# Down product of both feed-forward layers as seven block products instead of eight, with operand sums made on GpSimd

## What is computed

```python
D_MODEL, SEQ = 1024, 1024
FFN_HIDDEN = -(-8 * D_MODEL // (3 * 256)) * 256      # 2816

def swiglu(u, w_gate, w_up, w_down):
    return (jax.nn.silu(u @ w_gate) * (u @ w_up)) @ w_down
...
x = x + mixer(rmsnorm(x, g0));  x = x + swiglu(rmsnorm(x, g1), w_gate, w_up, w_down)
```

## Time and profile before

| what | value |
|---|---|
| median of 3 runs | 2556.0 us (2555.74 to 2561.59) |
| the profiled execution: its time | 2557.84 us |
| the profiled execution: its span | 2556.1 us |
| granted TensorE clock, mean over the span | 0.984 |
| TensorE busy | 2486.2 us (97%) |
| VectorE busy | 1537.7 us (60%) |
| ScalarE busy | 1011.0 us (40%) |
| GpSimd busy | 216.8 us (8%) |
| down phase of layer 0 | from 1288.9 to 1533.4 us |
| down phase of layer 1 | from 2288.3 to 2534.1 us |
| gate and up phases | up to 1288.9 and up to 2288.3 us, 20 rounds each |

### The profile page before, as it was taken

One profiled execution on the slowest core, in us unless ns is written; L12 is line 12 of the kernel. 1 busy time (PEld: TensorE's weight loads), 2 busy tenths in 40 slices (PEclk: granted clock), 3 DMA queues, 4 the chain that ended last, 5 costly groups with the idle time before them and its releaser, 6 DMA issues.

```text
span 2556.1 us, 34009 instructions
## 1 busy us (share of the span) xinstructions
PE 2486.2 (97%) x13110; PEld 1960.9 (77%) x13110; DVE 1537.7 (60%) x2635; ACT 1011.0 (40%) x1818; POOL 216.8 (8%) x243
## 2 busy tenths in 40 slices
PE   9999999999999999999999999989999999999998
PEld 6587778865658788888888787776878888888787
DVE  5489967846635775666543637637676665653454
ACT  5423234545434433333332434537443333332333
POOL 4025524310000000000100000000000000000000
PEclk9999979999999999999999999999999999999999
DMA  6121100010004322232364341110332222236342
GB/s 191 41 75 42 50 9 11 2 34 1 1 26 146 125 80 78 83 94 72 103 224 147 133 130 34 41 50 26 91 123 83 83 83 83 83 126 220 116 161 103
DMA packets 207184, 217.54 MB, mean 85 GB/s; under 512 B 12496, under 2 KB 174304, under 8 KB 203568
## 3 DMA queue, kind: packets, MB, share of 16 engines
q1 hardware_dynamic: 204080, 196.13, 24.6%
q0 software_dynamic: 2944, 19.24, 2.1%
HBM read 172.35 MB, written 42.47 MB: 84 GB/s over the span
## 4 chain that ended last, share of the span: by engine, by line
PE 90%; DVE 5%; ACT 3%; issue 2%; POOL 0%; DVEq 0%; ACTq 0%; POOLq 0%
PE ps L335 25%; PE ps L337 24%; PE ps L336 24%; PE ps L2956 3%; PE ps L2933 2%; PE ps L2944 1%; DVE met L2081 1%; PE ps L2320 1%; ACT d_p L1591 1%; PE ps L2334 1%; PE ps L2329 1%; PE ps L1863 1%; PE ps L2373 1%; PE ps L2297 1%; PE ps L2382 1%
## 5 line engine op out<-in xcount | busy, mean ns | idle before, releaser
L324 DVE TENSOR_TENSOR wlo<-wraw,whi 128x1024 fp32r<-128x1024 f32 x152 | 186.3, 1228 | 370.5 <-ACT whi L318 370.1
L318 ACT ACTIVATE whi<-wraw 128x1024 fp32r<-128x1024 f32 x166 | 175.0, 1055 | 356.7 <-PE ps L337 339.2
L335 PE MATMUL ps<-ahi,whi 128*128 128x512 f32 x704 | 276.2, 392 | 6.4 <-DVE hT L962 4.1
L337 PE MATMUL ps<-ahi,wlo 128*128 128x512 f32 x704 | 274.9, 390 | 0.0
L336 PE MATMUL ps<-alo,whi 128*128 128x512 f32 x704 | 274.7, 390 | 0.0
L335 PE MATMUL ps<-uhi,whi 128*128 128x512 f32 x608 | 245.0, 403 | 6.5 <-DVE ulo L494 3.4
L335 PE MATMUL ps<-q_T,whi 128*128 128x512 f32 x640 | 249.4, 390 | 1.6 <-ACT upr L763 1.6
L337 PE MATMUL ps<-q_T,wlo 128*128 128x512 f32 x640 | 249.3, 389 | 0.0
L336 PE MATMUL ps<-q_T,whi 128*128 128x512 f32 x640 | 249.3, 389 | 0.0
L335 PE MATMUL ps<-q_B,whi 128*128 128x512 f32 x608 | 239.1, 393 | 2.4 <-DVE q_B L494 2.4
L336 PE MATMUL ps<-ulo,whi 128*128 128x512 f32 x608 | 237.3, 390 | 0.0
(11 more groups left out here) (465 smaller groups left out, 4517.5 us busy)
## 6 DMA issues: line engine op xcount, KB each, us to landing
wraw<-in_ffn_w_down_dram SPq DMA_DIRECT2D x88, 512.0 KB, 3.7
wraw<-in_ffn_w_gate_dram SPq DMA_DIRECT2D x44, 512.0 KB, 5.5
araw<-acts SPq DMA_DIRECT2D x88, 256.0 KB, 3.8
wraw<-in_ab_w_in_dram SPq DMA_DIRECT2D x24, 512.0 KB, 3.8
park<-hT POOLq DMA_DIRECT2D x3, 4096.0 KB, 12.3
wraw<-in_ffn_w_up_dram SPq DMA_DIRECT2D x24, 512.0 KB, 5.2
acts<-sgA SPq DMA_DIRECT2D x12, 1024.0 KB, 4.6
raw<-in_ffn_w_up_dram SPq DMA_DIRECT2D x20, 512.0 KB, 4.0
```

What stands on the lines that cost most here:

```text
L318: nc.scalar.activation(as_raw(whi[:, t.slot, :]), raw, ACT.Copy).then_inc(S("w_high"), 1)
L324: eng.tensor_tensor(as_raw(wlo[:, t.slot, :]), raw, as_raw(whi[:, t.slot, :]).bitcast(F32), ALU.subtract).then_inc(S("w_split"), 1)
L335: nc.tensor.matmul(dst, wh, xh, start=start, stop=False, **kw)
L337: return nc.tensor.matmul(dst, wl, xh, start=False, stop=stop, **kw)
```

## The change

The down product is cut in blocks: the hidden tiles into even and odd ones of each pair (`a`), the output features into a low and a high half, the tokens into two halves. Eight block products (2 x 2 x 2) become seven, listed in `DOWN`: which weight block or sum of blocks, which activation block or sum, which of two sets of four banks, whether the banks start from zero, and which quarter of `hT` the banks are added to. A step now holds two hidden tiles of one block product: 512 output features of each, so the weight tile is 128 x (2 x 512) and the activation tile grows from 512 to 2 x 512. There are 7 x 6 = 42 steps (`DT`) in each layer; every sixth has only one hidden tile and half the work. The activations' ring is three slots like the weights'.

The four sums of a pair's weights and the four of its activations are made by GpSimd (`ffn_sums`), 11 pairs in each layer, during the gate and up phase: the weights of the pair are loaded from DRAM once more, summed in place and stored to `w_sums`; the activations are summed in place in `sg[p % 2]` after their store to `acts`, and stored to `act_sums`. ScalarE's `sum_copy` into that buffer then waits for this second store (`sums_stored`). Block products 0 and 1 use plain operands, 2 to 4 sums on both sides, 5 and 6 a sum on one side. `park` is loaded back behind steps 3 to 10.

VectorE now adds banks to `hT` seven times four in each layer, each after the second step of the following block product; the one exception is the sixth and seventh block product, which use the same set of banks.

```diff
-    return order + [("down", layer, h, k) for h in range(2) for k in range(HT)]
+    return order + [("down", layer, i, c) for i in range(len(DOWN)) for c in range(DC)]
+DOWN = (
+    ((0, 1, 0), (0, 1, 1), 0, True, (0, 1)),
+    ((0, 0, 0), (0, 0, 1), 1, True, (0, 1)),
+    ((1, 1, 1), (1, 0, 1), 0, True, (1, 0)),
+    ((1, 0, 0), (1, 1, 0), 1, False, (0, 0)),
+    ((1, 1, 0), (0, 1, 0), 0, False, (0, 0)),
+    ((1, 0, 1), (1, 0, 0), 1, False, (1, 0)),
+    ((0, 1, 1), (1, 1, 1), 1, False, (1, 1)),
+)
...
+DC = (PAIRS + 1) // 2
+DT = len(DOWN) * DC
+DOWN_BANKS = ((6, 7, 0, 1), (2, 3, 4, 5))
+SAME_PIECE = {1: 0, 4: 3, 5: 2}
...
-        araw = at("araw", [P, 4, HALF], 32 * KB)
-        ahi = at("ahi", [P, 4, HALF], 40 * KB, F32R)
-        alo = at("alo", [P, 4, HALF], 48 * KB, F32R)
+        araw = at("araw", [P, RING, D], 32 * KB)
+        ahi = at("ahi", [P, RING, D], 44 * KB, F32R)
+        alo = at("alo", [P, RING, D], 188 * KB, F32R)
+        wd = at("wd", [P, 2, D], 176 * KB)
...
+            lo, hi = slice(0, HALF), slice(HALF, D)
+            pool.wait_ge(*after("t_lo", 16 * layer + 16))
+            for p in range(PAIRS):
+                if p:
+                    pool.wait_ge(*weights_summed(layer, p - 1))
+                pool.dma_start(wd[:, :, :], down_v[layer][:, p, :, :]).then_inc(S("wd_landed"), 16)
+                pool.wait_ge(*after("wd_landed", 16 * (PAIRS * layer + p + 1)))
+                add(wd[:, 1, hi], wd[:, 0, hi], wd[:, 1, hi], ALU.add)
+                add(wd[:, 0, hi], wd[:, 0, lo], wd[:, 0, hi], ALU.subtract)
+                add(wd[:, 0, lo], wd[:, 1, hi], wd[:, 0, lo], ALU.subtract, 2)
+                add(wd[:, 1, lo], wd[:, 1, lo], wd[:, 0, lo], ALU.subtract, 1)
+                pool.wait_ge(*after("p_sum", n[0]))
+                pool.dma_start(w_sums[:, p, :, :], wd[:, :, :]).then_inc(S("w_summed"), 16)
+                v = sg[p % 2]
+                pool.wait_ge(*act_stored(layer, p))
+                add(v[:, 0, hi], v[:, 0, lo], v[:, 0, hi], ALU.subtract)
+                add(v[:, 0, lo], v[:, 1, lo], v[:, 0, lo], ALU.subtract)
+                add(v[:, 1, lo], v[:, 1, lo], v[:, 0, hi], ALU.subtract, 2)
+                add(v[:, 1, hi], v[:, 1, hi], v[:, 1, lo], ALU.subtract, 1)
+                pool.wait_ge(*after("p_sum", n[0]))
+                pool.dma_start(act_sums[:, p, :, :], v[:, :, :]).then_inc(S(f"act_sums{p % 2}"), 16)
...
+                if w_sum:
+                    sp_.wait_ge(*weights_summed(layer, pairs[-1]))
+                sp_.wait_ge(S("w_split"), tile.n + 1)
+                src = w_sums if w_sum else down_v[layer]
+                sp_.dma_start(as_pairs(wraw[:, tile.slot, 0:width]),
+                              src[:, pairs[0]:pairs[-1] + 1, w_odd, w_half * HALF:(w_half + 1) * HALF]
+                              ).then_inc(S(f"w_landed{tile.slot}"), 16)
+                if n < RING:
                     sp_.wait_ge(*after("s_prod", NC * layer + AT[("A11", NJ - 1)] + 1))
                 else:
-                    sp_.wait_ge(*after("a_lo", 2 * HT * layer + n - 3))
-                p = k // 2
-                sp_.wait_ge(*act_stored(layer, p))
-                sp_.dma_start(araw[:, n % 4, :], acts[:, k, h * HALF:(h + 1) * HALF]).then_inc(S(f"a_landed{n % 4}"), 16)
+                    sp_.wait_ge(*after("a_lo", DT * layer + n - RING + 1))
+                for p in pairs:
+                    if a_sum:
+                        sp_.wait_ge(*sums_stored(layer, p))
+                    else:
+                        sp_.wait_ge(*act_stored(layer, p))
+                src = act_sums if a_sum else acts_v
+                sp_.dma_start(as_pairs(araw[:, n % RING, 0:width]),
+                              src[:, pairs[0]:pairs[-1] + 1, a_odd, a_half * HALF:(a_half + 1) * HALF]
+                              ).then_inc(S(f"a_landed{n % RING}"), 16)
                 if n == 2:
                     store(PAIRS - 1)
-                if 4 <= n < 4 + KT:
-                    if n == 4:
+                if 3 <= n < 3 + KT:
+                    if n == 3:
                         sp_.wait_ge(*after("s_prod", NC * layer + AT[("S3", NJ - 1)] + 1))
-                    sp_.dma_start(hT[:, n - 4, :], park[:, n - 4, :]).then_inc(S("h_again"), 16)
+                    sp_.dma_start(hT[:, n - 3, :], park[:, n - 3, :]).then_inc(S("h_again"), 16)
...
+                pe.wait_ge(*after("a_lo", DT * layer + n + 1))
+                for q in range(len(pairs)):
+                    if i == len(DOWN) - 1 and c == 1 and q == 1:
+                        norm_whole(pe, 2 * norm + 2, DOWN_BANKS[0][0])
+                    cols = slice(q * HALF, (q + 1) * HALF)
+                    for m in range(4):
+                        if c == 0 and q == 0 and earlier:
+                            pe.wait_ge(*after("d_added", 4 * len(DOWN) * layer + 4 * earlier[-1] + m + 1))
+                        elif c == 0 and q == 0 and (i, m) == (0, 2):
+                            pe.wait_ge(*out_count(layer, "C12", NJ - 2))
+                        elif c == 0 and q == 0 and (i, m) == (1, 0):
+                            pe.wait_ge(*out_count(layer, "C12", NJ - 1))
+                        w = slice(q * HALF + m * P, q * HALF + (m + 1) * P)
+                        last = three_pass(bank(banks[m]), whi[:, tile.slot, w], wlo[:, tile.slot, w],
+                                          ahi[:, n % RING, cols], alo[:, n % RING, cols],
+                                          start and c == 0 and q == 0, c == DC - 1 and q == len(pairs) - 1,
+                                          skip_group_check=True)
+                        if c == DC - 1 and m < 3:
+                            last.then_inc(S("d_part"), 1)
+                last.then_inc(S("w_used"), 1)
...
-                    act.wait_ge(*act_stored(layer, p - 2))
+                    act.wait_ge(*sums_stored(layer, p - 2))
...
+            def h_add(i, m):
+                if m < 3:
+                    dve.wait_ge(*after("d_part", 3 * len(DOWN) * layer + 3 * i + m + 1))
                 else:
-                    tile_done(dve, down_tile(layer, HT * (h + 1) - 1))
-                rows = slice(h * HALF, (h + 1) * HALF)
-                dve.tensor_tensor(hT[:, m, rows], bank(BANK_M[m]), hT[:, m, rows], ALU.add).then_inc(S("d_added"), 1)
+                    tile_done(dve, down_tile(layer, DC * (i + 1) - 1))
...
+                if i in SAME_PIECE:
+                    dve.wait_ge(*after("d_added", 4 * len(DOWN) * layer + 4 * SAME_PIECE[i] + m + 1))
+                half, h = DOWN[i][4]
+                dst = hT[:, 4 * half + m, rows_of(h)]
+                dve.tensor_tensor(dst, bank(DOWN_BANKS[DOWN[i][2]][m]), dst, ALU.add).then_inc(S("d_added"), 1)
...
+            for n in range(3, last + 2):
                 down_low(n)
-            dve.wait_ge(*after("h_again", 16 * KT * (layer + 1)))
-            for m in range(KT):
-                h_add(0, m)
-                if m >= 2:
-                    norm_add(dve, 2 * norm, m - 1)
-                if m == 4:
-                    down_low(HT + 2)
+                if n % DC == 1:
+                    i = n // DC - 1
+                    if i == 0:
+                        dve.wait_ge(*after("h_again", 16 * KT * (layer + 1)))
+                    if i < 5:
+                        for m in range(4):
+                            h_add(i, m)
+                if n == last - DC + 2:
+                    for k in range(1, 4):
+                        norm_add(dve, 2 * norm, k)
+            for m in range(4):
+                h_add(5, m)
+                if m >= 1:
+                    norm_add(dve, 2 * norm, m + 3)
             norm_add(dve, 2 * norm, KT - 1)
-            down_low(HT + 3)
+            down_low(last + 2)
+            down_low(last + 3)
             norm_invert(dve, 2 * norm)
-            for n in range(HT + 4, 2 * HT):
-                down_low(n)
-                if n - HT - 4 < KT + 2:
-                    norm_step(dve, 2 * norm, n - HT - 4, last=layer == 1)
+            for k in range(KT + 2):
+                norm_step(dve, 2 * norm, k, last=layer == 1)
+                if k in (1, 3):
+                    down_low(last + 4 + k // 2)
...
             ffn_park(pool, 0)
+            ffn_sums(pool, 0)
             c_prepare(pool, *after("s_prod", AT[("A12", NJ - 1)] + 1))
             d_prepare(pool)
             ffn_park(pool, 1)
+            ffn_sums(pool, 1)
```

153 lines of the change are left out of this document (81 added, 72 removed).

## The result

The changed kernel takes 2512.1 us (median of 4 runs, 2510.9 to 2513.1) against 2556.2 us for the kernel before (2555.7 to 2561.6): ratio 0.982, 95% interval 0.9805 to 0.984, 44 us less. The whole interval lies under 1, so the gain is clear of the noise, though it is under 2%. The forecast was 2503, with a range of 2491 to 2526.

> The changed kernel once more, beside the others and the kernel before on one chip, as their measure. All theories: 2511 to 2515 us, with 9 us of idle before step 8 in layer 0 and 5 in layer 1, and a down product of 224 and 219 us in the two layers.

A forecast was written before the change was run, and what follows sets the result against it. TensorE, busy 97% of the span, was taken as the bound. -59.8 - 8.8 + 8.0 + 6.6 + 3.0 + 0.5 - 2.0 = -52.5 us took 2557.84 to 2505.3, given as 2503 for the median; range 2491 to 2526.

The forecast's parts named there:

- Part 1: Down phase matmuls: 924 instead of 1056 in each layer, 0.2267 us each, 59.8 us less.
- Part 2: Down phase: the old change of token halves goes, 4.4 us in each layer, 8.8 us less.
- Part 3: Down phase: the longer operand splits on ScalarE and VectorE, 2.1 and 2.5 us in a 5.44 us step, are hidden.
- Part 4: Before down step 8: `park` comes back late and TensorE stalls, 4.0 us in each layer with the restart, 8.0 more.
- Part 5: Step 36: sixth and seventh block product share banks, so TensorE waits for VectorE's adds, 3.3 us a layer, 6.6 more.
- Part 6: Gate and up phase: GpSimd's sums and VectorE keep each other out, 1.5 us in each layer, 3.0 more.
- Part 7: Ends of the layers: last sums of squares 0.5 us more after layer 0, 2.0 us less after layer 1.
- DMA is late at the start of the down phase: Rival, chance 0.10: weight loads behind `park` are late too, 5 us more in each layer, 2513.
- The rival of the lock: Rival, chance 0.05: half of a pair's 10.2 us hold-up reaches TensorE, 112 us instead of 3, 2612; slower.

The follow-up runs named there:

- E7: The changed kernel with the edits of E1, E2 and E3 together: 2487.8 us, ratio 0.9725 to the kernel before.
- E2: Against the changed kernel, VectorE adds the first block product to the residual after the split of step 10, not 7: 2494.2 us, ratio 0.9748 to the kernel before.
- E1: Against the changed kernel, GpSimd begins layer 0's small `c_prepare` loads only after VectorE's first residual add: 2507.0 us, ratio 0.9799 to the kernel before.
- E3: Against the changed kernel, VectorE adds the sixth block product ahead of the split of step 37: 2504.6 us, ratio 0.9792 to the kernel before.
- E5: The changed kernel with eight unused GpSimd adds more a pair, each waiting for the last but one: 2626.9 us, ratio 1.0266 to the kernel before.
- E9: The changed kernel with four unused GpSimd adds more a pair, each waiting for the last but one: 2525.9 us, ratio 0.9876 to the kernel before.
- E10: The changed kernel with E5's eight added adds a pair, each writing over its own first operand: 2622.8 us, ratio 1.0267 to the kernel before.
- E6: The kernel before with GpSimd's sums made and stored but used by nobody: 2559.8 us, ratio 1.0007 to the kernel before.
- E4: Against the changed kernel, the residual's pieces are fetched two a step at steps 3 to 6: 2496.9 us, ratio 0.9758 to the kernel before.
- E11: The changed kernel with the edits of E4 and E1 together: 2492.5 us, ratio 0.9742 to the kernel before.

## Why the prediction was right, and where not

The measured time, 2512.1, lies 9 us above the forecast and inside the range.

- **Part 1** (59.8 less): right. With every wait gone (E7) a down phase takes 209.6 us for 921 distances between matmuls and the matmul against ones, about 0.227 each.
- **Part 2** (8.8 less): a little low. The phases before took 243.7 and 245.1 us; E7's take 209.6, of which 132 matmuls less explain 29.9. That leaves 4.2 and 5.6, 9.8 in all.
- **Part 3** (hidden): right, E7 shows no wait for a split.
- **Part 4** (8.0 more): the mechanism was right, its size was the failing step: 11.1 and 6.6, 17.7 us by E2, with 9.2 us of idle in layer 0 where 5.3 was the most allowed for, and 4.7 in layer 1. The volume was right: from the store to the landing some 14.5 MB were moved in layer 0 (332 GB/s over 43.65 us) and 14.2 in layer 1 (359 over 39.5). Three things were missing. The rate: 400 GB/s was taken for all of it from 1290.55 on, but in both layers the first 7 us ran at 237 to 328 GB/s, and in layer 0 GpSimd's small loads, which the change shifts into this stretch, brought it down to 247 for some us; they were not in the sum, though `c_prepare` stands behind the sums in GpSimd's queue (3.8 us, E1). The issue: by the sum the last piece is issued 31.3 us after the phase's start and there after 39.3. In layer 1 it was issued after 31.3 and there after 40.8, in layer 0 after 34.2 and 45.2; issue to landing was 11.3 and 10.3 us in the median against 6.5 before. (14.2 MB at 400 GB/s from 1290.55 end at 1326.1, too, and not near 1328.) And the clock: behind the idle time TensorE ran at half the granted clock, 1.9 us in each layer, for 0.5 assumed.
- **Part 5** (6.6 more): right, 5.6 by E3 and 6.0 by E7 against E2. The first wait came at 1.6 us for 1.5 forecast. The other two were shorter than forecast, 0.27 and 0.23 for 0.7 and 0.5, and the cost besides the idle was larger, 0.7 to 0.9 us in each layer for 0.6, so part of the agreement is luck.
- **Part 6** (3.0 more): the lock is there in both directions, its price to TensorE is 0.0. The bounds, 0 and 224, were far apart, and the value near the lower end was still too high. The Trainium skill's rule (page "SBUF — State Buffer", section "Who interferes with whom", that the later of the two is blocked for a whole instruction) agrees with most of these rows: 1.78 us is 0.69 and a wait of 1.09, within one GpSimd add of 1.28. Its words "for the whole instruction" are too small for the 4.77 us in the changed kernel itself, and for E5, E9 and E10, where the wait lasted through four and eight instructions.
- **Part 7** (+0.5 and -2.0): about right in size, +0.8 and -1.3, but the runs don't show its mechanism. E6, whose down phase is the old one, also has 756.5 us between the phases, and the kernels E1 to E4, E7 and E11 have 754.6 to 755.8; the end is 20.1 us in one profile of the changed kernel and 21.4 in the other.

The sum over the parts as measured: -59.8 - 9.8 + 17.7 + 6.0 + 0 + 0.8 - 1.3 and 0.3 at the start of the down phase give -46.1, as the spans do, against -52.5. These 6.4 us are part 4 (9.7 too little), eased above all by parts 2 and 6. The other 2.7 of the 9 us come from the step to the median: the forecast took off 1.8 because the profiled execution before had been that much above its median, the changed kernel's was not, and the rest is mostly rounding. Of the rivals, "DMA is late at the start of the down phase" (2513) comes nearest, in part by luck: late transfers are the cause, but the rival blamed the steps' own weights, which E2 shows in time, and put 5 us on each layer where 7.1 and 2.6 were added. The rival of the lock needed 2.5 us a pair; it was 0 here. With E5's eight more adds it was 109 / 22 = 5.0 us a pair and the kernel came out slower than before, so that case was real at twice the work.

## What to carry to other kernels

When work is put ahead of others in an engine's queue, look at everything behind it, its DMA issues above all: loads in small pieces that were harmless in a quiet stretch cost 3.8 us in a full one. A wait that only a later step needs belongs behind the work that the next step needs; moving four adds by three steps gave back 17.7 us. Give GpSimd's adds beside a busy VectorE in short groups, each waiting for the one before, and look first at the start of a phase, where the reserve is small: a row of four cost 2.9 to 4.1 us there and next to nothing later.

## What the hardware showed

- A row of GpSimd adds, each free to start when the last ends, shut VectorE's two-operand instruction out for the whole row where it began straight behind GpSimd's own DMA issue: the instruction took 4.1 to 4.9 us for three adds, 5.3 to 6.0 for four, 10.3 to 11.0 for eight. Where GpSimd had waited for a DMA ahead of the row, it took 2.4 at most. With each added add waiting for the one before it, 2.3 us at most.
- After 9.2 and after 4.7 us of idle TensorE's granted clock was 0.50, and matmuls lay 0.43 us apart until it was 1.00 again. The wait of 1.6 us at 1480 left it at 1.00. In between both occurred: 0.50 after 2.25 us at 942, 1.00 after 2.22 us at 1931 (E9).
- The same DMA engines at a share over 1.0 moved 402 GB/s with loads in long pieces, 247 with GpSimd's small ones among them.
